# Differential attention heads: four woven streams replaced by a table of eight rounds

## What is computed

```python
for i in range(s // Q_BLOCK):                       # two blocks of 128 queries
    s0 = i * Q_BLOCK
    end = s0 + Q_BLOCK
    sc = jnp.einsum('bqhmd,bkhmd->bhmqk', q[:, s0:end], k_sh[:, :end])
    mask = jnp.arange(end)[None, :] <= (s0 + jnp.arange(Q_BLOCK))[:, None]
    p = jax.nn.softmax(jnp.where(mask, sc, -jnp.inf), axis=-1)
    a = p[:, :, 0] - lam * p[:, :, 1]
    outs.append(jnp.einsum('bhqk,bkhe->bqhe', a, v_sh[:, :end]))
```

## Time and profile before

| | us |
|---|---|
| median of 3 runs | 3013.38 |
| lowest, highest | 3011.24, 3013.92 |
| the profiled execution | 3013.77 |
| its span (first to last instruction) | 3011.6 |
| busy: TensorE, VectorE, ScalarE, GpSimd | 2782.8, 1884.4, 1244.5, 778.7 |
| block of heads 0 to 3 (from T0 to T8) | 1128.77 to 1186.17 |
| block of heads 4 to 7 (from T10 to the last head's output) | 1193.44 to 1252.75 |

### The profile page before, as it was taken

The page is one execution under the profiler, slowest core; times in us unless marked ns, Lnnn a source line. Parts: engine busy times, 40 slices in busy tenths (PEclk is TensorE's granted clock), DMA queues, the critical chain, the costliest instruction groups (busy, mean ns, idle before and its releaser), DMA issues.

```text
span 3011.6 us, 43694 instructions
## 1 busy us (share of the span) xinstructions
PE 2782.8 (92%) x17592; PEld 2511.7 (83%) x17592; DVE 1884.4 (63%) x3243; ACT 1244.5 (41%) x1739; POOL 778.7 (26%) x340
## 2 busy tenths in 40 slices
PE   8989999999999987699999999999799858898998
PEld 7869999999888865499999988888798746776896
DVE  5655997776555565559977765555654675415554
ACT  3434463334544544334633344445444412132443
POOL 0001986664000001009876630000000230042000
PEclk9999999999999998799999999999899977789999
DMA  5554554445666642245544456666456410023454
GB/s 198 161 181 153 172 181 146 141 140 168 190 193 190 192 147 92 69 143 173 182 155 141 141 168 190 192 192 191 138 182 190 131 57 25 1 82 99 157 183 145
DMA packets 122889, 449.51 MB, mean 149 GB/s; under 512 B 13712, under 2 KB 13840, under 8 KB 122560
## 3 DMA queue, kind: packets, MB, share of 16 engines
q1 hardware_dynamic: 120800, 439.47, 46.2%
q0 software_dynamic: 1888, 7.23, 0.8%
HBM read 445.60 MB, written 1.05 MB: 148 GB/s over the span
## 4 chain that ended last, share of the span: by engine, by line
PE 82%; DVE 13%; ACT 2%; POOL 2%; issue 1%; DMA 0%; DVEq 0%; SPq 0%; ACTq 0%
PE ps L423 11%; PE ps L424 11%; PE ps L425 11%; PE ps L473 10%; PE ps L475 10%; PE ps L474 10%; DVE W L1271 10%; PE ps L542 4%; PE ps L662 3%; PE ps L445 2%; PE ps L446 2%; PE ps L447 2%; DVE x L1271 1%; POOL lo L1929 1%; PE ps L409 1%
## 5 line engine op out<-in xcount | busy, mean ns | idle before, releaser
L898 ACT ACTIVATE hi<-ring 128x1024 fp32r<-128x1024 f32 x830 | 878.9, 1059 | 1260.2 <-PE ps L425 651.8
L1294 DVE TENSOR_TENSOR lo<-ring,hi 128x1024 fp32r<-128x1024 f32 x540 | 660.8, 1225 | 601.6 <-ACT hi L898 601.5
L423 PE MATMUL ps<-xT_r,hi 128*128 128x256 f32 x3248 | 936.7, 288 | 11.9 <-POOL lo L1929 8.1
L424 PE MATMUL ps<-xT_r,hi 128*128 128x256 f32 x3248 | 921.7, 284 | 0.0
L425 PE MATMUL ps<-xT_r,lo 128*128 128x256 f32 x3248 | 921.4, 284 | 0.0
L1929 POOL TENSOR_TENSOR lo<-ring,hi 128x1024 fp32r<-128x1024 f32 x290 | 732.8, 2534 | 669.8 <-ACT hi L898 669.8
L423 PEld LDWEIGHTS ps<-xT_r,hi 128*128 128x128 f32 x3248 | 626.2, 193 | 16.2 <-POOL lo L1929 5.4
L424 PEld LDWEIGHTS ps<-xT_r,hi 128*128 128x128 f32 x3248 | 626.6, 193 | 0.7 <-issue 0.7
L425 PEld LDWEIGHTS ps<-xT_r,lo 128*128 128x128 f32 x3248 | 625.9, 193 | 0.0
L473 PE MATMUL ps<-hi,oht_r 128*128 128x512 f32 x1040 | 411.5, 396 | 13.0 <-DVE W L1271 13.0
L475 PE MATMUL ps<-hi,oht_r 128*128 128x512 f32 x1040 | 409.3, 394 | 0.0
(11 more groups left out here) (216 smaller groups left out, 2896.8 us busy)
## 6 DMA issues: line engine op xcount, KB each, us to landing
ring<-in_peer_u SPq DMA_DIRECT2D x256, 512.0 KB, 3.6
ring<-in_peer_v SPq DMA_DIRECT2D x256, 512.0 KB, 4.3
ring<-in_f SPq DMA_DIRECT2D x132, 512.0 KB, 3.6
ring<-in_ret_vg SPq DMA_DIRECT2D x32, 512.0 KB, 3.6
ring<-in_peer_q SPq DMA_DIRECT2D x32, 512.0 KB, 3.5
ring<-in_ret_qk SPq DMA_DIRECT2D x16, 512.0 KB, 4.3
ring<-in_ret_out SPq DMA_DIRECT2D x16, 512.0 KB, 3.8
ring<-in_in_shift SPq DMA_DIRECT2D x14, 512.0 KB, 4.3
```

Of the source, the lines that this page charges most:

```text
L423: pe.matmul(o, h, xT[:, k, 0:256], start=k == 0, stop=False)
L424: pe.matmul(o, h, xT[:, k, 256:512], start=False, stop=False)
L898: hid.done(a.activation(hi[m % NH][:, :], ring[j % NR][:, :], ACT.Copy), j)
L1294: lo_v.done(v.tensor_tensor(lo[m % NH][:, :], ring[j % NR][:, :], as32(hi[m % NH][:, :]), ALU.subtract), j)
```

## The change

The four streams, woven as generators, become a table of eight rounds, written out in the same way in all three programs. `diff_turn(nb, n)` names the heads whose scores TensorE makes in round n: streams (1, 0) and (0, 1) start in round 0, stream (1, 1) in round 1, stream (0, 0) in round 2, and each stream's second head follows three rounds after its first. So the rounds have two heads, one late head, one early head, two heads, one late head, one early head, none, none.

In round n TensorE transposes the weights of the heads of round n - 2, does the tile step, does the outputs of the heads of round n - 2, and then the scores of round n. ScalarE copies the transposed weights of round n - 2, takes the exponentials of round n - 1, makes the high part for the tile step, and copies the outputs of round n - 2. VectorE does mask and maxima and then the weights of the heads of round n - 1, and the tile step's low part behind them. So a whole round of TensorE lies between the scores of a head and the transposition of its weights, and the tile lies between that and the head's output. The waits for the turned queries and keys stand ahead of the first round's tile on TensorE. Buffers, banks, instructions and their number stay as they are.

```diff
--- before.py
+++ after.py
@@ -383,6 +383,11 @@
+        def diff_turn(nb, n):
+
+            streams = ((1, 0, 0), (1, 1, 1), (0, 0, 2), (0, 1, 0))
+            return [(tt, u, nb * 4 + u * 2 + m) for tt, u, o in streams for m in range(2) if o + 3 * m == n]
+
@@ -570,38 +575,47 @@   (tensor_program)
-                def heads(nb, tt, u):
-                    s, p, a2, aT, mx, ss = D_hd[tt, u]
+                def scores(tt, u, h):
                     own = (tt * 2 + u,)
-                    for _ in range(tt + u):
-                        yield
                     kw = 128 * (tt + 1)
+                    b = bank("diff_s", tt, h, among=own)
...
+                def weights(tt, u, h):
+                    a2 = D_hd[tt, u][2]
+                    b = bank("diff_t", tt, h, among=(tt * 2 + u,))
+                    pe.wait_ge(*at(dve, "diff_a", tt, h))
...
+                def outputs(tt, u, h):
+                    aT = D_hd[tt, u][3]
+                    ob = bank("diff_o", tt, h, among=(tt * 2 + u,))
+                    pe.wait_ge(*at(act, "diff_aT", tt, h))
+                    pe.wait_ge(*at(act, "diff_p", 2, h // 4, tt))
...
+                def rounds(nb, tiles):
                     for z in ("diff_q", "diff_k"):
                         pe.wait_ge(*at(dve, z, "Tn", nb * 4))
                         pe.wait_ge(*at(act, z, "Tn", nb * 4 + 2))
...
+                    for n in range(8):
+                        for w in diff_turn(nb, n - 2):
+                            weights(*w)
+                        next(tiles, None)
+                        for w in diff_turn(nb, n - 2):
+                            outputs(*w)
+                        for w in diff_turn(nb, n):
+                            scores(*w)
...
-                weave([tiles_b()] + [heads(0, tt, u) for u in range(2) for tt in range(2)])
+                rounds(0, tiles_b())
...
-                weave([tiles_c()] + [heads(1, tt, u) for u in range(2) for tt in range(2)])
+                rounds(1, tiles_c())
@@ -1020,25 +1034,34 @@   (scalar_program)
...
+                def rounds(nb, tiles):
+                    for n in range(8):
+                        for w in diff_turn(nb, n - 2):
+                            weights(*w)
+                        for w in diff_turn(nb, n - 1):
+                            exps(*w)
+                        next(tiles, None)
+                        for w in diff_turn(nb, n - 2):
+                            outputs(*w)
```

More of the change, by code:

```diff
@@ new lines, in weights, with exps, outputs @@
+                def weights(tt, u, h):
+                    kw = 128 * (tt + 1)
+                    a.wait_ge(*at(mm, "diff_t", tt, h))
+                    act.done(a.activation(D_hd[tt, u][3][:, 0:kw], ps("diff_t", tt, h)[:, 0:kw], ACT.Copy), "diff_aT", tt, h)
+                    empties(act, "diff_t", tt, h)
+                def exps(tt, u, h):
+                    s, p, a2, aT, mx, ss = D_hd[tt, u]
+                    softmax(("diff", tt, h), s, p, 128 * (tt + 1), mx, ss)
+                def outputs(tt, u, h):
+                    o, sq = ps("diff_o", tt, h)[:, 0:128], D_sq[:, (tt * 8 + h) * 128:(tt * 8 + h) * 128 + 128]
+                    n = tt * 4 + h % 4
+                    a.wait_ge(*at(mm, "diff_av", tt, h))
+                    act.done(a.activation(D_o[:, tt, h * 128:h * 128 + 128], o, ACT.Copy))
+                    act.done(a.activation(sq, o, ACT.Square, accum_out=D_rr[h // 4][:, n:n + 1]), "diff_o", h // 4)
+                    empties(act, "diff_o", tt, h)
```

66 lines of the change are left out of this document (25 added, 41 removed).

## The result

| | before | after |
|---|---|---|
| median, us | 3013.65 (3011.24 to 3017.69, 4 runs) | 2976.11 (2975.09 to 2984.21, 4 runs) |
| the profiled execution, its span | 3013.77, 3011.6 | 2975.66, 2973.9 |

The ratio is 0.988, 95% interval 0.986 to 0.990: 37.5 us less by the medians, 37.7 by the spans. The forecast was 2981.4, range 2973 to 2991. The time lies in the range, but some 6 us of the gain lie in a stretch of unchanged code that is as short in versions without the edit, and the stage itself gained 27.8 us where I had summed 32.0.

What follows compares the result with a forecast made beforehand. TensorE bounds the kernel, standing 28.6 us before transpositions until VectorE has the weights, then running at half clock. Block 0's 13.0 and block 1's 19.0 us saved make 32.0: 3013.4 - 32.0 = 2981.4 us, range 2973 to 2991.

Steps and rivals of the forecast that it cites:

- round 7: In block 0, TensorE waits some 3.7 us for the last early head's weights, behind VectorE's rotation stopped by GpSimd.
- the late head of block 1's round 3: In block 1's tile-less third round, TensorE waits 2.8 us for weights of the single head on tokens 128 to 255.
- block 1: Second changed stretch, heads 4 to 7: 59.3 us before, 40.3 forecast, 19.0 less.
- Rival D: The round in between doesn't cover; only high and low part leave the chain: about 10 us, 3003; chance 0.05.
- E: Slower: TensorE stands in each round for that round's own chain; both blocks about +6 us, 3019; chance 0.04.
- Rival B: GpSimd's holds (4.8 us) and the half-clock tiles (3.1 us) don't show in the blocks: 2973; chance 0.20.
- T5's: GpSimd's low part of this block 0 weight tile comes when VectorE is done with its round.
- block 0: First changed stretch, heads 0 to 3: 57.4 us before, 44.4 forecast, 13.0 less.
- T3: Block 0 weight tile whose GpSimd low part stops the second head's weights in round 1; TensorE waits 2.7 us.
- rival C: Pauses that are left still bring the clock down in most rounds: three more, 8.4 us, 2989; chance 0.19.
- O0: Block 1's first output tile: waits 1.9 us for turned outputs, then runs at half clock, 1.7 us more.
- T7: Block 0's last weight tile: mostly at half clock after the 3.7 us wait, 1.4 us.

Runs made afterwards that it cites:

- e4: Kernel before, with VectorE doing the heads first and the tile's low part behind them, nothing else: 2999.76 us, ratio 0.9958.
- e3: Kernel after, with three of block 0's four GpSimd low parts moved to VectorE: 2977.62 us, ratio 0.988.
- e6: Kernel before, with six tiny fills added on VectorE behind block 1: 3012.33 us, ratio 1.000.
- e9: Kernel before, with only the streams' starting rounds and order taken from the table: 3012.72 us, ratio 1.0005.
- e5: Kernel after, with weights transposed one round earlier, behind that round's tile, so no round in between: 2994.14 us, ratio 0.9941.
- e2: Kernel after, with VectorE's rotation of the queries' second half moved two tiles on, behind the last weights: 2974.29 us, ratio 0.988.

## Why the prediction came out

**Right in which waits are left.** The signs named beforehand: waits for L594 10.0 us (about 13 forecast), the longest at round 7 and at the late head of block 1's round 3 as said, clock of the blocks 0.93 and 0.92 (0.95). Rival D (only the high and low part leave the chain) is e4, and it stops at 8.8 us of the stage; E would have needed rounds of 7.2 us, they take 46.92 / 8 = 5.9 and 42.08 / 8 = 5.3. Rival B had no stops: they are there, with nearly my numbers, 2.20 (2.7 forecast) and 3.67 (3.7). (B's price of 4.8 took the whole 2.7 for the stop, though my own sum left 0.2 to 0.5 of it to the pair; e3 leaves 0.26.) T5's didn't show, as forecast. The Trainium skill's page "SBUF — State Buffer", section "Who interferes with whom", says that a VectorE instruction on two SBUF inputs and a GpSimd instruction that reads SBUF shut each other out. The two rows above agree (2.31 for 0.35, 3.27 for 1.27). One row fits the other direction: GpSimd's own low part took 2.60 at 1161.77 instead of 2.34, having met a VectorE weights instruction that ran until 1162.12.

**The waits were sized well.** Forecast: block 0 7.8 us (0.9 + 2.7 + 0.5 + 3.7), block 1 8.3 (0.9 + 0.8 + 2.8 + 1.9 + 0.9 + 0.5 and 0.5 of a pair), together 16.1. Measured as idle time: 8.0 and 7.7, together 15.6. The largest misses are 0.5 (T3, and the late head in block 1's round 3: 2.34 for 2.8).

**The work at a slower clock was sized too small.** The stage's sum was 44.4 + 40.3 = 84.7 us; it takes 46.92 + 42.08 = 89.0. The idle part being 0.5 less, the busy part is 4.8 more than my 65.5 + 3.1 = 68.6. Three terms:
- T2, behind the stop at T3. I let a tile run at half clock only after the pauses of over 3 us. From 1140.31 to 1144.68 it took 4.37 us for 2.85, clock 0.62 from 1140.3 to 1144.7: 1.5. I had the row for a price and had rival C for it, but no such tile in my own sum.
- O0, behind 2.34 and 2.02 us of waiting: 1200.25 to 1205.31, 5.06 us, 2.2 more than at full clock where I took 1.7. T7, 1169.62 to 1173.78, cost 1.3 (1.4 forecast).
- TensorE's own work, 2.9. From its start to the next start, weights times values took 0.53 us for a late head and 0.32 for an early one in the rows below, where scores follow; I had read 0.36, with a tile behind it, and 0.2 from the earlier trace rows. Four of each in two blocks, with 0.75 for a pair, make some 2 us of it. The rest is small differences, such as 2.93 to 2.96 us for a tile with scores behind it.

```profile
1149.44 0.60 PE L603 MATMUL ps<-W 128*128 128x128 f32 x4
1149.97 0.70 PE L582 MATMUL ps<-W 64*128 64x256 f32 x2
...
1154.86 0.39 PE L603 MATMUL ps<-W 128*128 128x128 f32 x2
1155.18 0.70 PE L582 MATMUL ps<-W 64*128 64x256 f32 x2
```

The scores were right (a late head alone 1.39 for 1.3, a pair 1.96 for 2.0).

**What made up for it.** My sum let nothing happen outside the stage. There 9.9 us went (37.7 - 27.8), of which 6.1 are the mixer's, and e4, e6 and e9, which have no table, have the short mixer too. Without the mixer's 6.1 the time would stand at about 2982, within a us of the forecast; that is luck of two errors as well, since 4.2 too much in the stage and 3.8 not foreseen elsewhere cancel.

**Where the argument was wrong although the number held.** I wrote that the round in between would take away waits, and counted the clock only behind the pauses that I saw left. By e5 the round covers the pairs but opens other waits, and nets 1.1 us of idle time (34.4 without it, 33.3 with it); what it is worth are the falls of the clock behind the rounds with two heads, 9.5 us of TensorE's work. The idle time went with the order of VectorE and ScalarE and with the table (13.5 us from before to e5).

## What to carry to other kernels

Before giving a chain more cover, take out of it what needn't be in it: another order on the engines beside it (weights ahead of low part, exponentials ahead of high part) was worth 13.4 of the 27.8 us. Ask of each pause whether the clock falls behind it: e5 and after have nearly the same idle time, but in after the falls behind three double pauses of 1.7 us are gone, and TensorE's work is 9.5 us shorter. Look at each new order for what GpSimd's instructions now run beside: in every version here but e3 some VectorE instruction of block 0 was stopped, by up to 2.1 us. Judge an edit of a few us by the stretch that it touches, since unchanged stretches moved by 6 us.

## What was not expected of the hardware

- The length of a pause doesn't tell its price. Behind one of 2.20 us the first seven of T2's twelve products ran at half clock (0.62 over the tile, 1.5 us); behind one of 3.67 us T7 began at full clock and fell only 1.2 us into it (1.3 us). In e5 two pauses of 0.90 and 0.83 us were followed by a clock of 0.52, and a single one of 1.87 us ahead of T7 by 1.00.
- The stop between VectorE and GpSimd takes hold of `SCALAR_TENSOR_TENSOR` with two SBUF inputs (2.31 for 0.35), of the rotation's `TENSOR_TENSOR` (3.27 for 1.27 for four), and of `TENSOR_SCALAR` on one SBUF tensor (1.26 for 0.17 in e2, 2.25 for 0.35 in the earlier trace rows). In e2 the mask from PSUM and the maxima, between 1162.48 and 1163.36, ran beside the same GpSimd instruction at their usual 0.42 us each.
- A stretch of 190 us with unchanged code takes 189.5 to 195.9 us, at granted clocks of 0.84 to 0.80, and the whole unchanged kernel moves between executions in steps of about 6 us.
